# Plain fp32 in place of high and low fp32r parts, in the gather, the scatter and the shares of an expert stage

## The reference

```python
    scores = jax.nn.sigmoid((t @ w_router).astype(jnp.float32))
    sel = scores + router_bias.astype(jnp.float32)
    ...
    _, idx = lax.top_k(jnp.where(in_group, sel, -jnp.inf), TOP_K)
    top_s = jnp.take_along_axis(scores, idx, axis=-1)
    gate = top_s / jnp.sum(top_s, -1, keepdims=True)
    combine = jnp.sum(jax.nn.one_hot(idx, N_EXPERTS, dtype=jnp.float32) * gate[..., None], 1)
    hg = jnp.einsum('td,edf->tef', t, w_gate)
    hu = jnp.einsum('td,edf->tef', t, w_up)
    act = jax.nn.silu(hg) * hu * combine[..., None].astype(t.dtype)
    y = jnp.einsum('tef,efd->td', act, w_down)
```

## Time and profile before

| | |
|---|---|
| median of 3 runs | 1542.32 us (1539.61 to 1542.69) |
| the profiled execution | 1542.35 us |
| its span in the profile | 1540.5 us |
| moe0: first gather to the end of the last down product | 281.8 to 405.5 us |
| moe1 | 664.0 to 787.8 us |
| moe2 | 942.5 to 1155.3 us |
| moe3 | 1311.7 to 1524.3 us |
| busy: TensorE, VectorE, ACT, POOL | 1433.6, 542.8, 335.5, 147.8 us |
| mean granted clock of TensorE | 0.966 |

### The profile page before, as it was taken

The page is one execution under the profiler, slowest core; times in us unless marked ns, Lnnn a source line. Parts: engine busy times, 40 slices in busy tenths (PEclk is TensorE's granted clock), DMA queues, the critical chain, the costliest instruction groups (busy, mean ns, idle before and its releaser), DMA issues.

```text
span 1540.5 us, 16133 instructions
## 1 busy us (share of the span) xinstructions
PE 1433.6 (93%) x6724; PEld 820.7 (53%) x6724; DVE 542.8 (35%) x1077; ACT 335.5 (22%) x732; POOL 147.8 (10%) x103
## 2 busy tenths in 40 slices
PE   6999999799899999879989998999988998999995
PEld 3686884354378788435436444434435764444432
DVE  2591245523565124542251133121014353312113
ACT  3103231321211323132123132101102342211111
POOL 1008820000002920000000000000000000000000
PEclk8999999899899999989989998999998999999998
DMA  9996352999667641399946558799999407799995
GB/s 377 412 383 253 132 205 113 372 399 428 245 240 287 265 157 63 135 385 394 426 178 241 207 219 327 322 427 428 427 428 408 166 0 326 288 430 427 428 428 239
DMA packets 36875, 462.55 MB, mean 300 GB/s; under 512 B 4120, under 2 KB 6440, under 8 KB 8216
## 3 DMA queue, kind: packets, MB, share of 16 engines
q1 hardware_dynamic: 34112, 448.91, 71.2%
q0 software_dynamic: 1648, 10.39, 1.7%
q10 hardware_dynamic: 1032, 2.10, 0.7%
HBM read 458.24 MB, written 3.15 MB: 299 GB/s over the span
## 4 chain that ended last, share of the span: by engine, by line
PE 86%; DVE 5%; DMA 5%; ACT 2%; issue 1%; SPq 0%; DVEq 0%; ACTq 0%
PE work L847 19%; PE work L654 13%; PE work L899 10%; PE work L637 8%; PE acc L654 7%; PE acc L637 5%; DMA ring<-in_stream 5%; PE work L801 5%; PE acc L881 3%; PE work L646 3%; PE work L1357 2%; PE acc L1502 2%; PE work L1148 1%; PE acc L1170 1%; DVE stat L2214 1%
## 5 line engine op out<-in xcount | busy, mean ns | idle before, releaser
L847 PE MATMUL work<-ring,area 128*64 128x512 f32 x864 | 196.5, 599 | 3.2 <-DMA ring<-in_stream 3.2
L847 PEld LDWEIGHTS work<-ring,area 128*64 128x64 f32 x864 | 63.5, 138 | 122.8 <-issue 117.8
L654 PE MATMUL work<-ht_sb,ring 128*128 128x256 f32 x576 | 126.3, 380 | 0.6 <-ACT ht_sb L1683 0.6
L654 PEld LDWEIGHTS work<-ht_sb,ring 128*128 128x128 f32 x576 | 109.0, 190 | 17.7 <-issue 2.3
L654 PE MATMUL acc<-ht_sb,ring 128*128 128x256 f32 x512 | 114.0, 381 | 0.0
L2581 DVE SCALAR_TENSOR_TENSOR area<-area,comb_slot,work 128x256 f32<-128x256 f32 (+1 forms) x32 | 19.7, 614 | 262.2 <-ACT area L1788 262.2
L654 PEld LDWEIGHTS acc<-ht_sb,ring 128*128 128x128 f32 x512 | 96.1, 190 | 14.8 <-issue 2.0
L637 PE MATMUL work<-ring,ht_sb 128*128 128x512 f32 (+1 forms) x224 | 95.3, 586 | 4.2 <-ACT ht_sb L1683 2.6
L847 PE MATMUL work<-area 128*64 128x512 f32 x400 | 90.7, 594 | 2.3 <-DMA area<-in_stream 2.3
L2601 DVE TENSOR_TENSOR area_r<-work,area_r 128x512 fp32r<-128x512 f32 x64 | 44.3, 692 | 137.7 <-ACT area_r L1799 109.7
L899 PE MATMUL work<-ring,area 128*64 128x512 f32 x384 | 87.5, 597 | 0.0
(11 more groups left out here) (360 smaller groups left out, 1911.0 us busy)
## 6 DMA issues: line engine op xcount, KB each, us to landing
ring<-in_stream SPq DMA_DIRECT2D x136, 2048.0 KB, 13.0
area<-in_stream SPq DMA_DIRECT2D x46, 2048.0 KB, 12.0
cst<-in_stream SPq DMA_DIRECT2D x14, 2048.0 KB, 15.3
early<-in_stream SPq DMA_DIRECT2D x14, 2048.0 KB, 21.2
ln_sb<-in_ln_vecs POOLq DMA_DIRECT2D x8, 1024.0 KB, 11.6
rel_rows<-mt_sb ACTq DMA_DIRECT2D x1, 2048.0 KB
area<-in_stream SPq DMA_DIRECT2D x2, 1024.0 KB, 10.4
mt_sb<-in_stream SPq DMA_DIRECT2D x2, 1024.0 KB, 16.3
```

The source lines that it names most:

```text
L654: ins = pe.matmul(dst, w[:, k, c0:c0 + n], src[:, k0 + k, :], start=k == 0, stop=k == ks - 1)
L847: ins = pe.matmul(banks[half][e * CAP:(e + 1) * CAP, :], tokens[:, k, at:at + CAP], w[:, e, half * W:(half + 1) * W], start=k == 0, stop=k ...
```

## The change

Tokens, shares and results stay in plain fp32, and the gather, the shares and the scatter are plain fp32 matmuls of them. The high and low parts go, with the steps that make them (ACT's two `high_part` and, in moe0 and moe1, all of its Y copies; POOL's and VectorE's `low_part`; VectorE's Y_LO). In moe0 and moe1 VectorE's scaling writes Y itself. In moe2 and moe3 ACT copies the first half of Y, VectorE the second. The scatter waits for one semaphore for each half. The shares are 16 columns in place of 32, and VectorE copies them in place of adding. The core of the diff:

```diff
                 def gather(double, kk, bank):
 
                     pe.wait_ge(sel_ready, 4 * number + double + 1)
-                    parts = [(x_part, t) for x_part in (X_HI, X_LO) for t in range(TT)]
-                    steps = [(k, n) for k in range(2) for n in range(4)]
...
-                    for i, (k, n) in enumerate(steps):
-                        if first and i == 6:
-                            pe.wait_ge(x_lo_ready, TT * (number + 1))
-                        x_part, t = parts[n]
+                    for k in range(2):
                         c = (2 * kk + k) * P
-                        ins = pe.matmul(bank[:, k * 4 * CAP:(k + 1) * 4 * CAP], x_part[:, t, c:c + P],
-                                        SEL[:, t, double * 4 * CAP:(double + 1) * 4 * CAP], start=n == 0 and not (first and k), stop=n == 3 and (k == 1 or not first))
+                        for t in range(TT):
+                            ins = pe.matmul(bank[:, k * 4 * CAP:(k + 1) * 4 * CAP], XN[:, t, c:c + P],
+                                            SEL[:, t, double * 4 * CAP:(double + 1) * 4 * CAP], start=t == 0, stop=t == TT - 1)
                     ins.then_inc(gathered, 1)
...
-                            ins = pe.matmul(bank[:, p * 2 * NE:(p + 1) * 2 * NE], SEL[:, t, p * 2 * CAP:(p + 1) * 2 * CAP],
-                                            COMB_PARTS[:, t, :], start=t == 0, stop=t == TT - 1)
+                            ins = pe.matmul(bank[:, p * NE:(p + 1) * NE], SEL[:, t, p * 2 * CAP:(p + 1) * 2 * CAP],
+                                            route_comb[:, t, :], start=t == 0, stop=t == TT - 1)
...
                     for n in ns:
-                        pe.wait_ge(y_lo_ready, 2 * (before_pairs + p) + n + 1)
+                        pe.wait_ge(y_ready[n], before_pairs + p + 1)
                         for t in range(TT):
-                            for part in (Y_HI, Y_LO):
-                                ins = pe.matmul(acc[2 * n + t][:, :], BACK[:, p, t * P:(t + 1) * P], part[:, n, :],
-                                                start=p == 0 and part is Y_HI, stop=p == PAIRS - 1 and part is Y_LO)
+                            ins = pe.matmul(acc[2 * n + t][:, :], BACK[:, p, t * P:(t + 1) * P], Y[:, n, :],
+                                            start=p == 0, stop=p == PAIRS - 1)
...
-                    act.activation(Y_HI[:, 0, :], banks[0][:, :], ACT.Copy).then_inc(y_hi_ready, 1)
...
-                    act.activation(Y_HI[:, 1, :], banks[1][:, :], ACT.Copy).then_inc(y_hi_ready, 1)
+                        act.activation(Y[:, 0, :], work[3 if p % 2 else 1][:, :], ACT.Copy).then_inc(y_ready[0], 1)
...
-                        dve.wait_ge(y_hi_ready, 2 * (before_pairs + p) + n + 1)
-                        dve.tensor_tensor(Y_LO[:, n, :], banks[n][:, :], Y_HI[:, n, :], ALU.subtract).then_inc(y_lo_ready, 1)
+                    if number < DEPTH:
+                        dve.wait_ge(half_summed, before_pairs + p + 1)
+                        dve.tensor_tensor(Y[:, 0, :], banks[0][:, :], GAIN[:, 1, 0:W], ALU.mult).then_inc(y_ready[0], 1)
+                    dve.wait_ge(*slot_free(SLOTS[MOE_NAMES[number]] + (p + 1) * pair_slots(fc) - 1))
+                    if number < DEPTH:
+                        dve.tensor_tensor(Y[:, 1, :], banks[1][:, :], GAIN[:, 1, W:2 * W], ALU.mult).then_inc(y_ready[1], 1)
+                    else:
+                        dve.tensor_copy(Y[:, 1, :], banks[1][:, :]).then_inc(y_ready[1], 1)
```

More of the change, by code:

```diff
@@ L270, in build @@
         x_sb, ln_sb = (sb(n, 2 * D) for n in ("x_sb", "ln_sb"))
-        (xn_sb, xn_r), (ht_sb, ht_r), (mt_sb, mt_r) = (sb_twin(n, 2 * D) for n in ("xn_sb", "ht_sb", "mt_sb"))
+        xn_sb, ht_sb = (sb(n, 2 * D) for n in ("xn_sb", "ht_sb"))
+        mt_sb = sb("mt_sb", 2 * D)
         cst, cst_r = sb_twin("cst", N_CONST + 2 * D)
@@ L447, in build @@
             sem(n) for n in ("silu_ready", "act_ready", "act_flipped", "act_t_ready"))
[L448 to L449 removed]
+        half_summed = sem("half_summed")
+        y_ready = [sem("y_first_ready"), sem("y_second_ready")]
         def overflow_sems(name):
@@ L790, in gather @@
                     pe.wait_ge(sel_ready, 4 * number + double + 1)
-                    parts = [(x_part, t) for x_part in (X_HI, X_LO) for t in range(TT)]
-                    steps = [(k, n) for k in range(2) for n in range(4)]
-                    first = double == 0 and kk == 0
-                    if first:
-                        steps = [(k, n) for k in range(2) for n in range(3)] + [(k, 3) for k in range(2)]
-                    for i, (k, n) in enumerate(steps):
-                        if first and i == 6:
-                            pe.wait_ge(x_lo_ready, TT * (number + 1))
-                        x_part, t = parts[n]
+                    for k in range(2):
                         c = (2 * kk + k) * P
-                        ins = pe.matmul(bank[:, k * 4 * CAP:(k + 1) * 4 * CAP], x_part[:, t, c:c + P],
-                                        SEL[:, t, double * 4 * CAP:(double + 1) * 4 * CAP], start=n == 0 and not (first and k), stop=n == 3 and (k == 1 or not first))
+                        for t in range(TT):
+                            ins = pe.matmul(bank[:, k * 4 * CAP:(k + 1) * 4 * CAP], XN[:, t, c:c + P],
+                                            SEL[:, t, double * 4 * CAP:(double + 1) * 4 * CAP], start=t == 0, stop=t == TT - 1)
                     ins.then_inc(gathered, 1)
-                pe.wait_ge(x_hi_ready, TT * (number + 1))
-                pe.wait_ge(x_lo_ready, TT * number + 1)
+                pe.wait_ge(x_scaled, TT * (number + 1))
                 for kk in range(2):
@@ L921, in all_tokens @@
                     steps = 2 * fc
-                    pe.wait_ge(y_lo_ready, 2 * (before_pairs + PAIRS))
+                    for n in range(2):
+                        pe.wait_ge(y_ready[n], before_pairs + PAIRS)
                     for t in range(TT):
-                        pe.wait_ge(rest["rest_ready"], t + 1)
                         for half in range(2):
@@ L930, in all_tokens @@
                         pe.wait_ge(rest["comb_spread"], t + 1)
-                    pe.wait_ge(rest["rest_ready"], TT + 1)
+                    pe.wait_ge(rest["rest_ready"], 1)
                     over_comb = route[:, 8 * 32:9 * 32].rearrange("p (t n) -> p t n", t=TT)
@@ L966, in moe @@
                             banks = [work[1], work[2]] if p % 2 else [work[2], work[3]]
-                            pe.wait_ge(y_lo_ready, 2 * (before_pairs + p))
+                            for n in range(2):
+                                pe.wait_ge(y_ready[n], before_pairs + p)
                         for h in range(2):
@@ L1729, in scale_tokens @@
                 act.activation(XN[:, t, :], X[:, t, :], ACT.Identity, bias=token[:, 6 + t:7 + t], scale=rstd[:, t:t + 1])\
-                   .then_inc(act_chain, 1)
-                C.made(act_chain)
-            def high_part(t):
-                act.wait_ge(act_chain, C.own[act_chain.name])
-                act.activation(X_HI[:, t, :], XN[:, t, :], ACT.Copy).then_inc(x_hi_ready, 1)
+                   .then_inc(x_scaled, 1)
             def parts(t):
@@ L2545, in experts @@
                 select(0)
-                low_part(number)
                 dve.wait_ge(counted, 2 * number + 2)
@@ L2565, in slot_combs @@
                         a = e * CAP
-                        src = bank[a:a + CAP, first * 34:last * 34].rearrange("p (a b) -> p a b", b=34)
-                        ins = dve.tensor_reduce(comb_slot[a:a + CAP, first:last], src[:, :, e:e + NE + 1:NE], AX, ALU.add)
+                        src = bank[a:a + CAP, first * 18:last * 18].rearrange("p (a b) -> p a b", b=18)
+                        ins = dve.tensor_copy(comb_slot[a:a + CAP, first:last], src[:, :, e])
                     ins.then_inc(comb_slot_ready, 1)
@@ L2606, in all_tokens @@
                     over_comb = rt(8)
-                    for t in range(TT):
-                        dve.tensor_tensor(XN[:, t, :], X_HI[:, t, :], X_LO[:, t, :], ALU.add).then_inc(rest["rest_ready"], 1)
                     dve.tensor_scalar(over_comb, place, CAP + 0.5, None, ALU.is_gt).then_inc(rest["product"], 1)
```

59 lines of the change are left out of this document (10 added, 49 removed).

## The result

| | before | after |
|---|---|---|
| median | 1542.5 us (1539.6 to 1542.9) | 1630.6 us (1626.9 to 1631.1) |
| ratio | | 1.057, 95% interval 1.055 to 1.059 |
| profiled execution and its span | 1542.35 and 1540.5 us | 1626.86 and 1625.0 us |

A forecast was written before the change was run, and what follows sets the result against it. The prediction took TensorE, busy for 93% of the span, to bound the kernel. Moe0 and moe1 added 48.0 us, moe2 and moe3 38.3: +86.3 on 1542.35, so 1629 us, range 1614 to 1641.

The forecast's parts named there:

- Two records for a plain matmul: TensorE: each plain fp32 matmul gives two trace records, 0.432 us at 256 columns and 0.86 at 512.
- some 110: Expected busy time in us of the gather's x512 records, and likewise of the scatter's x256, in the profile after.
- Gathers 12.6: Every expert stage: two gathers in a row cost +1.57 us, 8 times, so +12.6 us a stage.
- scatters 10.7: Scatters in moe0 and moe1 ahead of the stage's end: +5.5, +3.9 and +1.3 us for half scatters.
- Shares 1.7: Shares by place: 16 plain matmuls of 16 columns replace 16 fp32r ones of 32, +1.7 us a stage.
- The waits for weights go: moe2 and moe3: TensorE's waits for weights, 4.1 us each, vanish before work is added, +20.0 us a stage.
- The ends: Behind the last down product, less splitting work: moe0 and moe1 -1.05 us each, moe2 -1.7, moe3 0.
- branches may stall: Range term: as the program gets shorter, other taken branches may cross a page and stall, +5 us.
- the fetch of 5.22 us: moe2's end: ACT's idle "issue" at its branch, kept at 5.22 us but starting 1.7 us earlier.
- Exactly four times: Rival: each plain matmul costs four fp32r ones in the same place, +105 us, 1647 us; chance 0.05.
- the weights hide it: Rival: in moe2 and moe3 late transfers hide the extra work, +56.5 us, 1599 us; chance 0.05.
- one record: Rival: one record for one plain matmul of these shapes, -10.9 us, 1531 us; chance 0.03.

The follow-up runs named there:

- less to load: 23 of 48 weight slots of moe2 and of moe3 loaded by half: kernel before 1531.7 us, kernel after 1630.2 us.
- the second profile: The kernel after, unchanged, profiled a second time: 1630.3 us, ratio 1.056.
- without the branch: Branch and path for more tokens than a place list holds left out: of the kernel after 1625.6 us, of the kernel before 1538.1 us.
- pair 7 alone: The kernel before with a plain fp32 scatter for pair 7 only, all else in parts: 1535.6 us, ratio 0.9955.
- the scatters alone: The kernel before with only the scatters in plain fp32, gathers and shares in fp32r parts: 1570.2 us, ratio 1.018.
- the shares back: The kernel after with the shares by place back in two fp32r parts, gathers and scatters plain: 1618.7 us, ratio 1.048.
- the shares twice: The kernel after with each product of the shares made twice in a row into the same place: 1653.4 us, ratio 1.071.
- the gathers alone: The kernel before with only the gathers in plain fp32, shares and scatters in fp32r parts: 1581.6 us, ratio 1.025.

## Why the prediction was right, step by step

**Two records for a plain matmul, and its price from rows.** Right. x512, x256 and x128 came as counted; +1.57 for two gathers and +0.79 for a half scatter came to the hundredth (two gathers take 0.19 us more than their records' price before and after alike). The 129 and 121 us of busy time of gather and scatter are above my "some 110", which was 512 x 0.216 and 256 x 0.429 for records that overlap; the price never hung on it.

**Gathers 12.6, scatters 10.7 a stage.** Right by themselves: 12.9 and 12.2, 10.8 and 10.9 in moe0 and moe1.

**Shares 1.7.** Right as the records' cost (undone: 1.6 to 1.8 in the stages without a fall). What was missing is the fall of the clock behind them, a down product 1.7 us longer once in each profile, and that the first gathers of a stage do not cost the same each time: at the lower clock and while it rises 16 records took 5.1 to 6.7 us, where I had priced them like the rest.

**The waits for weights go, and nothing else is hidden.** Right: +20.4 in moe2 and moe3 for 20.0, and less to load changes nothing after.

**The ends.** Wrong in each of the first three stages, which cancelled in part. That the sum came within 2 us of the measured one is partly luck: in the second profile, which lies at the median, what was put at nothing ahead of moe0 is +1.8 us, the stages to their down products are 1.6 us dearer than forecast, and the ends give 1.8 us more (-5.6 for -3.8).
- moe0: -1.05 expected, 0.0 measured, and +2.2 in the second profile. The mechanism is right: without the branch (and with pair 7 alone) VectorE's second sum comes 2.89 us behind the down product, 0.84 us earlier than before. The kernel after loses 2.0 us at TensorE's branch, which I had only as a bound ("branches may stall"). In the first profile it gets 1.1 back in the block behind, which I did not follow; in the second it loses another 1.7 at the low clock right behind the stall.
- moe1: -1.05 expected, -4.2 measured. I let the sum end at VectorE's residual. TensorE's idle time there shrank, and a low clock in the block that follows was gone. Before, in moe1 and in moe2:

```profile
794.37 1.97 PE L676 MATMUL acc<-cst,xn_sb 128*128 128x128 f32 x8 [1.92 <-DVE xn_sb L2233]
796.86 10.14 PE L637 MATMUL work<-ring,ht_sb 128*128 128x512 f32 x16 [0.53 <-DVE x_sb L2267]
...
1163.75 1.97 PE L676 MATMUL acc<-cst,xn_sb 128*128 128x128 f32 x8 [5.83 <-DVE xn_sb L2233]
1166.24 9.78 PE L637 MATMUL work<-ring,ht_sb 128*128 128x512 f32 x16 [0.52 <-DVE x_sb L2267]
```

After, in moe1:

```profile
844.79 1.11 PE L665 MATMUL acc<-cst,xn_sb 128*128 128x128 f32 x8 [1.12 <-DVE xn_sb L2197]
847.29 7.13 PE L626 MATMUL work<-ring,ht_sb 128*128 128x512 f32 x16 [1.38 <-DVE x_sb L2231]
```

The same 16 records take 7.13 us at full clock; 3.0 of the 4.2 us are this. It repeated in the second profile, and without the branch and with less to load. But the shorter idle time is not all of the cause. With the same 1.12 us of it ahead of the transposes, the product took 8.63 us with the scatters alone, 8.70 with the shares back, 8.83 with pair 7 alone and 9.78 with the shares twice; with 1.90 to 1.92 us it took 8.58 us with the gathers alone and 10.03 to 10.14 in the four other profiles. What else decides it was not tested.
- moe2: -1.7 expected, -3.6 measured: VectorE's reciprocal came 2.6 us earlier, and the product behind it took 8.72 us for 9.78. I had kept the fetch of 5.22 us at its length and it was 4.35.
- moe3: 0 expected, +0.2 measured.

**The rivals.** "Exactly four times" asked for 1647, "the weights hide it" for 1599, "one record" for 1531: the measured prices, the halved load and the counts exclude one each. The first has a slip in its working: its own terms give +29.5 us in moe0 and moe1 and not +28.7, and its sum, +105, is that of 29.5. The bounds of the range add up to +17 and so to 1646 us, not to 1641; neither changes the outcome. A plain matmul costs 0.432 / 0.118 = 3.7 fp32r ones here, so the rule of the Trainium skill, "FP8 and Floating Point Precision", section "TensorE Precision Notes" (four passes), is right in kind and 8 to 9% high if it is taken as an exact price of four fp32r matmuls.

**Left open.** The part ahead of moe0 differs by up to 2.2 us between profiles of the same instructions (281.4 to 283.6 us for the first gather); I didn't follow it. Nor is it known which property of the plain shares brings the clock down, why it does so in one stage and not in the next, or what besides the idle time sets the clock in the block behind a stage.

## What to carry to other kernels

Count a matmul's records before you price it: where half as many matmuls leave as many records, nothing is saved, and here splitting into two fp32r parts is cheaper on TensorE than one plain fp32 (2 x 0.118 for 0.432 us). It is the other way where the splitting itself is the path, as for the last pair of a stage: use the plain form only there. And a sum over a stage should run on into the first product behind it, and be checked in a second profile. There TensorE's idle time taken away went along with up to 3.0 us more by the clock (moe1 of the kernel after), and elsewhere with next to nothing: in moe2 of the kernel before without the branch the idle time fell from 5.83 to 2.86 us and the product only from 9.78 to 9.56.

## What I had not expected of the hardware

- A row of 24 plain records of 16 columns, with TensorE busy throughout, is followed in 5 of 20 stages by a stretch at the lower clock (a down product of 5.14 to 5.35 us for 3.65), a row of 48 in 4 of 4; a row of 12 fp32r records of 32 columns in none of 28. In the kernel after the fall came in just those stages whose clock had risen early.
- One and the same taken branch costs TensorE 2.0 to 2.1 us in moe0 or nothing, from one program to the next, and ACT 1.8 to 5.7 us behind moe2 and moe3. An edit to another stretch of the program moves this, and ACT's part differed (4.35 and 2.57 us) between two executions of one program.
- Loading a quarter less left a stage in which the transfers were busy for 1.01 of the time, at 427 GB/s, exactly as long as it was.
